# First layer of a two-block transformer on one core: order of the modulation slabs, early loads and turnings changed

## The reference

```python
mod_x = (jax.nn.silu(c) @ w_ada[l] + b_ada[l])[:, None, :]          # w_ada: 1024 x 6144
mod_c = (jax.nn.silu(c_ctx) @ w_ada[l] + b_ada[l])[None, None, :]
sh_a, sc_a, g_a, sh_m, sc_m, g_m = jnp.split(mod_x, N_MOD, axis=-1)
hx = _modulate(_rmsnorm(x, norm_attn[l]), sh_a, sc_a)               # h * (1 + scale) + shift
hc = _modulate(_rmsnorm(cx, norm_attn[l]), csh_a, csc_a)            # the context, 256 rows
qa, ka, va, qb, kb, vb, ga, gb = proj(hx)                           # w_in: 1024 x 4352
cqa, cka, cva, cqb, ckb, cvb, cga, cgb = proj(hc)
# heads of q and k are normed and rotated; keys and values of x and context are joined
ya = _sweep_query_blocks(_gqa_attend, qa, ka_all, va_all)
yb = _sweep_query_blocks(lambda qq, kk, vv: _diff_attend(qq, kk, vv, lam), qb, kb_all, vb_all)
x = x + g_a * _merge(ya, yb, ga, gb, w_oa[l], w_ob[l], w_out[l])
hx = _modulate(_rmsnorm(x, norm_mlp[l]), sh_m, sc_m)
x = x + g_m * moe(hx.reshape(b * s, d)).reshape(b, s, d)            # 32 experts, top 4
```

## Time and profile before

| what | value |
|---|---|
| median of 3 runs | 1993.06 us (1991.01 to 1995.98) |
| profiled execution | 1986.67 us, span 1984.9 us, mean granted clock 0.979 |
| PE busy | 1817.4 us, 92% |
| VectorE busy | 773.5 us, 39% |
| ACT busy | 600.0 us, 30% |
| chain that ended last | PE 57%, DMA 32% (nearly all of it the experts' `w_up`) |
| moved from HBM | 560.58 MB, 283 GB/s over the span |

### The profile page before, as it was taken

One profiled execution on the slowest core, in us unless ns is written; L12 is line 12 of the kernel. 1 busy time (PEld: TensorE's weight loads), 2 busy tenths in 40 slices (PEclk: granted clock), 3 DMA queues, 4 the chain that ended last, 5 costly groups with the idle time before them and its releaser, 6 DMA issues.

```text
span 1984.9 us, 24817 instructions
## 1 busy us (share of the span) xinstructions
PE 1817.4 (92%) x10349; PEld 1120.8 (56%) x10349; DVE 773.5 (39%) x1348; ACT 600.0 (30%) x1070; POOL 31.9 (2%) x67
## 2 busy tenths in 40 slices
PE   3799988899999999999999999979899998899999
PEld 3687767433333333333333333338689997778998
DVE  2465636322222222222231321234554455645544
ACT  3345553211101101111111110135554445555442
POOL 1300001000000000000000000000000000000000
PEclk9899999799999999999999999989999999999999
DMA  8420758299999999999999999975236454324551
GB/s 303 156 101 21 265 183 338 77 428 427 430 427 427 426 428 428 427 427 428 428 429 427 427 428 427 427 277 205 100 120 212 171 180 180 116 97 149 191 174 40
DMA packets 122051, 563.28 MB, mean 284 GB/s; under 512 B 7216, under 2 KB 53424, under 8 KB 97360
## 3 DMA queue, kind: packets, MB, share of 16 engines
q1 hardware_dynamic: 118352, 557.86, 70.1%
q10 hardware_dynamic: 3584, 3.79, 0.6%
HBM read 560.58 MB, written 1.05 MB: 283 GB/s over the span
## 4 chain that ended last, share of the span: by engine, by line
PE 57%; DMA 32%; DVE 4%; ACT 3%; issue 2%; ACTq 1%; SPq 0%; DVEq 0%
DMA ring<-in_w_up 32%; PE ps L984 13%; PE ps L617 12%; PE ps L618 11%; PE ps L619 11%; PE ps L642 1%; PE ps L1017 1%; DVE part L1856 1%; PE ps L1108 1%; PE ps L724 1%; ACT part L1341 1%; DMA ring<-in_w_ob 1%; PE ps L734 1%; DVE arena L1856 1%; SPq L605 0%
## 5 line engine op out<-in xcount | busy, mean ns | idle before, releaser
L617 PE MATMUL ps<-part,part 128*128 128x256 f32 (+2 forms) x1592 | 512.5, 322 | 16.0 <-DVE part L1856 14.5
L618 PE MATMUL ps<-part,part 128*128 128x256 f32 (+2 forms) x1592 | 504.2, 317 | 0.0
L619 PE MATMUL ps<-part,part 128*128 128x256 f32 (+2 forms) x1592 | 503.5, 316 | 0.0
L984 PE MATMUL ps<-ring,arena 128*64 128x512 f32 x2048 | 456.3, 598 | 51.0 <-DMA ring<-in_w_up 51.0
L1856 DVE TENSOR_TENSOR part<-ring,part 128x1024 fp32r<-128x1024 f32 (+2 forms) x299 | 313.3, 1090 | 150.0 <-ACT part L1341 149.6
L984 PEld LDWEIGHTS ps<-ring,arena 128*64 128x64 f32 x2048 | 155.4, 137 | 349.7 <-issue 349.7
L617 PEld LDWEIGHTS ps<-part,part 128*128 128x128 f32 (+1 forms) x1592 | 306.6, 193 | 47.5 <-issue 20.8
L619 PEld LDWEIGHTS ps<-part,part 128*128 128x128 f32 (+1 forms) x1592 | 305.8, 192 | 19.7
L618 PEld LDWEIGHTS ps<-part,part 128*128 128x128 f32 (+1 forms) x1592 | 306.4, 192 | 17.5
L1341 ACT ACTIVATE part<-ring 128x1024 fp32r<-128x1024 f32 (+2 forms) x299 | 271.7, 947 | 46.3 <-PE ps L619 23.9
L1853 DVE TENSOR_SCALAR arena<-ps 64x512 f32<-64x512 f32 x128 | 88.1, 688 | 399.3 <-PE ps L984 394.3
(11 more groups left out here) (247 smaller groups left out, 1012.9 us busy)
## 6 DMA issues: line engine op xcount, KB each, us to landing
ring<-in_w_gate SPq DMA_DIRECT2D x64, 2048.0 KB, 17.0
ring<-in_w_up SPq DMA_DIRECT2D x64, 2048.0 KB, 21.7
ring<-in_w_down SPq DMA_DIRECT2D x64, 2048.0 KB, 19.1
ring<-in_ffn_w_in SPq DMA_DIRECT2D x44, 1024.0 KB, 7.8
ring<-in_w_ada SPq DMA_DIRECT2D x12, 2048.0 KB, 8.4
ring<-in_ffn_w_out SPq DMA_DIRECT2D x10, 2048.0 KB, 7.9
ring<-in_w_in SPq DMA_DIRECT2D x8, 2048.0 KB, 11.0
ring<-in_a_w_in SPq DMA_DIRECT2D x6, 2048.0 KB, 12.4
```

The costliest lines, as they stand in the source:

```text
L617: e.matmul(out, x[0], y[0], start=first, stop=False, skip_group_check=True)
L618: e.matmul(out, x[0], y[1], start=False, stop=False, skip_group_check=True)
L619: return e.matmul(out, x[1], y[0], start=False, stop=last, skip_group_check=True)
L984: i = e.matmul(PS[p + h][CAP * r:CAP * r + CAP, :], xg[:, k0 + k, :], W(("moe_" + "gu"[r], ex, k0))[:, k, 512 * h:512 * h + 512], start=False,
```

## The change

- SP's list: slabs 1 and 3 come before `qa`; `ob` comes before slab 9, the first slab of `w_out` before slab 11; slots of `w_out`, the experts and the later stages are renamed.
- Products 9, 10 and 11 stand at steps 32, 35 and 37 (31, 33 and 35 before). The row for `g_a` is made at step 36 and in other banks.
- Products 1 and 3 stand together behind the first piece; the second piece of kva is the second step and not the fourth. PE waits for each low quarter of the modulated rows as it needs it.
- Product 0 stands in front of the turning of x, product 2 between those of x and of the context.
- ACT issues `par` first and only four loads; the six small ones are issued by SP behind `vb`. Silu comes first on ACT.
- The context is modulated by ACT, not POOL.
- Turnings of queries and keys are one step later (last number of a line of `procs`), and ACT makes its high half ahead of the root in steps that norm heads.

```diff
             if slot is None:
-                slot = (0, 3, 2, 1)[next(turn) % 4]
+                slot = (2, 3, 1, 0)[next(turn) % 4]
...
-        for key in (("ada", 0, 0), ("ada", 2, 1), ("in", "kva"), ("in", "qa"), ("ada", 1, 0), ("ada", 3, 1), ("in", "kb"), ("in", "qb"),
+        for key in (("ada", 0, 0), ("ada", 2, 1), ("in", "kva"), ("ada", 1, 0), ("ada", 3, 1), ("in", "qa"), ("in", "kb"), ("in", "qb"),
...
-                    ("ada", 7, 2), ("o", "oa", 1), ("ada", 8, 2), ("ada", 9, 2), ("ada", 10, 2), ("o", "ob", 0), ("ada", 11, 2),
-                    ("out", 0, 2), ("first", 0, 4), ("out", 1, 1)):
+                    ("ada", 7, 2), ("o", "oa", 1), ("ada", 8, 2), ("o", "ob", 0), ("ada", 9, 2), ("ada", 10, 2), ("out", 0, 1), ("ada", 11, 2),
+                    ("first", 0, 4), ("out", 1, 0)):
...
-            for k0, slots in ((0, (4, 0)), (4, (3, 5))):
+            for k0, slots in ((0, (4, 2)), (4, (3, 5))):
...
-            for k0, slot in ((0, 2), (4, 1)):
+            for k0, slot in ((0, 1), (4, 0)):
...
-        a_order = [("kva", 0), ("qa0", 0), ("qa1", 0), ("kva", 1), ("qa0", 1), ("qa1", 1)]
+        a_order = [("kva", 0), ("kva", 1), ("qa0", 0), ("qa1", 0), ("qa0", 1), ("qa1", 1)]
...
-        procs = [("kva", 0, 2, 1, 4, 5), ("kva", 1, 2, None, 4, 5), ("qa0", 0, 4, 0, 5, 6), ("qa1", 0, 4, 0, 6, 7), ("kb0", 0, 4, 3, 8, 9),
+        procs = [("kva", 0, 2, 1, 4, 6), ("kva", 1, 2, None, 4, 6), ("qa0", 0, 4, 0, 5, 7), ("qa1", 0, 4, 0, 6, 8), ("kb0", 0, 4, 3, 8, 10),
...
-        ada_step = {4: 20, 5: 23, 6: 25, 7: 27, 8: 29, 9: 31, 10: 33, 11: 35}
+        ada_step = {4: 20, 5: 23, 6: 25, 7: 27, 8: 29, 9: 32, 10: 35, 11: 37}
...
+                if key == ("in", "vb"):
+                    e.dma_start(bdn[:, :], A["b_down"][0]).then_inc(*s_small_ld.up("bdn"))
...
+                            if t < 6 and q == 0 and k % 2 == 0:
+                                e.wait_ge(*s_ulo.of("a", who, 2 * p + k // 2))
...
                 if u == 0:
-                    for i in (2, 3):
-                        e.wait_ge(*s_nte.of(i))
+                    e.wait_ge(*s_nte.of(7))
...
-                if t == 1:
+                if t == 0:
                     ada(1, 6)
-                if t == 2:
+                    ada(3, 7)
                     ada_columns(1, 6, a.rows[1])
-                    ada(3, 7)
                     ada_columns(3, 7, a.rows[3])
...
+            e.wait_ge(*s_par.of())
+            e.wait_ge(*s_zero.of())
+            e.activation(a.c32[:, :, 0:2], P("c2", 0, 16).rearrange("p (k t) -> p k t", t=2), ACT.Silu).then_inc(*s_silu.up())
+            e.preload_act_table(ACT.Sqrt)
...
+                for k in (2 * p, 2 * p + 1):
+                    n = e.activation(a.uT[:, 1, k, :], a.uT[:, 1, k, :], ACT.Identity, bias=M(0, k, 1), scale=a.ga1[:, 8 + k:9 + k])
+                n.then_inc(*s_umodc.up(p))
...
+                if now:
+                    high_a(t + 4)
                 for i in now:
                     heads_root(i)
```

More of the change, by code:

```diff
@@ L605, in sync_program @@
                     e.dma_start(to, src).then_inc(s_slot[slot].sem, 16)
+                if key == ("in", "vb"):
+                    e.dma_start(bdn[:, :], A["b_down"][0]).then_inc(*s_small_ld.up("bdn"))
+                    e.dma_start(rw[:, :, :], A["router_w"][0].rearrange("(k p) n -> p k n", p=128)).then_inc(*s_small_ld.up("rw"))
+                    e.dma_start(rb[:, :], A["router_b"].broadcast_to([128, NE])).then_inc(*s_small_ld.up("rb"))
+                    e.dma_start(wgt[:, :, :], A["a_w_in"][0].rearrange("(k p) n -> p k n", p=128)[:, :, 3072:3080]
+                                ).then_inc(*s_small_ld.up("wgt"))
+                    e.dma_start(pos[:, :], A["positions"]).then_inc(*s_small_ld.up("pos"))
+                    e.dma_start(par[:, PCOL["b_gate"]:NP], A["par"][:, PCOL["b_gate"]:NP]).then_inc(*s_small_ld.up("biases"))
             for q in range(2):
@@ L622, in part @@
                 return [x[:, at:at + n] for x in w]
-            e.wait_ge(*s_con.of())
-            for who, rows in enumerate((X, a.cx)):
-                for q in range(2):
-                    e.wait_ge(*s_diag.of("first", who, q))
-                    for j in range(2):
-                        if who:
-                            e.wait_ge(*(s_urawd if j else s_uraw).of(0, q))
-                        for k in range(4):
-                            i = e.matmul(PS[2 * q + j][:, 128 * k:128 * k + 128], rows[:, q, 512 * j + 128 * k:512 * j + 128 * k + 128],
-                                         a.first_diag[who][q], start=True, stop=True, skip_group_check=True)
-                        i.then_inc(*s_ut.up("first", who, q, j))
             def ada(s, bank):
@@ L654, in tensor_program @@
             ada(0, 4)
-            ada(2, 5)
+            e.wait_ge(*s_con.of())
+            for who, rows in enumerate((X, a.cx)):
+                for q in range(2):
+                    e.wait_ge(*s_diag.of("first", who, q))
+                    for j in range(2):
+                        if who:
+                            e.wait_ge(*(s_urawd if j else s_uraw).of(0, q))
+                        for k in range(4):
+                            i = e.matmul(PS[2 * q + j][:, 128 * k:128 * k + 128], rows[:, q, 512 * j + 128 * k:512 * j + 128 * k + 128],
+                                         a.first_diag[who][q], start=True, stop=True, skip_group_check=True)
+                        i.then_inc(*s_ut.up("first", who, q, j))
+                if who == 0:
+                    ada(2, 5)
             ada_columns(0, 4, a.rows[0])
@@ L1388, in u_high, with context_mod @@
                 copy(u_of[who][:, 0, 2 * p:2 * p + 2, :], a.uT[:, who, 2 * p:2 * p + 2, :]).then_inc(*s_uhi.up("a", who, p))
-            ada_row(0, 4, a.rows[0])
-            ada_row(2, 5, a.rows[2])
-            high_a(0)
-            for who in range(2):
-                for p in range(2):
-                    u_high(who, p)
-            high_a(1)
-            ada_row(1, 6, a.rows[1])
-            high_a(2)
-            ada_row(3, 7, a.rows[3])
-            high_a(3)
-            high_a(4)
-            for who in range(2):
-                for p in range(2, 4):
-                    u_high(who, p)
-            for t in range(5, 8):
+            def context_mod(p):
+                e.wait_ge(*s_gain.of(p // 2))
+                if p >= 2:
+                    for q in range(2):
+                        e.wait_ge(*s_urawd.of(1, q))
+                else:
+                    e.wait_ge(*s_uraw.of(1, 1))
+                for k in (2 * p, 2 * p + 1):
+                    n = e.activation(a.uT[:, 1, k, :], a.uT[:, 1, k, :], ACT.Identity, bias=M(0, k, 1), scale=a.ga1[:, 8 + k:9 + k])
+                n.then_inc(*s_umodc.up(p))
+            for g in range(2):
+                ada_row(g, 4 + 2 * g, a.rows[g])
+                ada_row(2 + g, 5 + 2 * g, a.rows[2 + g])
+                high_a(g)
+                for p in (2 * g, 2 * g + 1):
+                    context_mod(p)
+                    u_high(0, p)
+                for p in (2 * g, 2 * g + 1):
+                    u_high(1, p)
+            for t in range(2, 8):
                 high_a(t)
@@ L1498, in scalar_program @@
                     e.preload_act_table(ACT.Sin)
-                if t + 4 < 50:
+                if t + 4 < 50 and not now:
                     high_a(t + 4)
@@ L1905, in vector_program @@
                     n.then_inc(*s_umod.up(p))
-                low_a(3 * g)
+                low_a(g)
                 for who in range(2):
@@ L1909, in vector_program @@
                         u_low(who, p)
-                if g == 0:
-                    low_a(1)
-                    low_a(2)
-            for t in range(4, 8):
+            for t in range(2, 8):
                 low_a(t)
```

50 lines of the change are left out of this document (15 added, 35 removed).

## The result

The changed kernel takes 1972.69 us (median of four runs, 1971.33 to 1973.61) against 1992.03 us for the kernel before beside it (1987.5 to 1996.0). The ratio is 0.9903, 95% interval 0.9881 to 0.9926: 19 us faster, where 15 were forecast. The profiled execution of the changed kernel took 1973.61 us, its span is 1971.6 us; the span before was 1984.9.

A forecast was written before the change was run, and what follows sets the result against it. Experts' weight loads bound 387 to 1297 us and only shift with PE's first layer; 17.9 + 2.6 - 5.2 = 15.3 us off 1986.67 gives 1971.4, carried to a median of 1978 us, range 1964 to 1988.

The forecast's parts named there:

- Start: PE's start: bound moves from ACT's queue to slab 0, landing at 17.3; first projection piece at 36.1 against 46.19.
- Rival (b): At the start, only 9 to 10 us of gain stay, giving 1988 us; chance 0.19 together with (d).
- Second half of the modulation: kva's second half at 53.8, not 74.35 (20.5 us); kb at 73.7 against 91.8; 17.9 us gained so far, start included.
- Turnings: Turning keys and queries a step later removes 3.3 us of PE's waits, less 0.7 at first attention: 2.6 us gained.
- Rival (c): VectorE's two normed-row buffers make it wait for later turnings, costing PE about 30 us: 2008 us; chance 0.06.
- Small loads and POOL: Small loads on SP may hold it 15 us, and ACT modulates the context instead of POOL: nothing gained or lost.
- Late products: ob's wait and slow product go (10.3 us); waits of 4.8 and 7.4 at slabs 9 and 11 come: 5.2 us lost.
- (a): The late slabs don't end last, so the gain is 30.8 us and the time 1962 us; chance 0.17.
- (d): ob is still late and its 8.6 us wait stays as well: 1988 us; chance 0.19 together with Rival (b).
- the last line of the sum: Carries the profiled execution's 1971.4 us to a median of 1977.8, as the earlier profile was 6.4 us under its median.

The follow-up runs named there:

- small_on_act: The changed kernel with its six small loads moved from SP back to ACT's queue, behind the four first ones: 1981.14 us, ratio 0.9950 to the kernel before.
- second_old: The changed kernel with the second half of the modulation, its loads and piece order as before: 1978.39 us, ratio 0.9948 to the kernel before.
- turn_back: The changed kernel with keys and queries turned one step sooner, as before: 1973.80 us, ratio 0.9916 to the kernel before.
- late_only: The kernel before with only the change's late part (order of late loads, products 9 to 11, gain row) laid on it: 1996.48 us, ratio 1.0036.
- early_only: The changed kernel with its late part (order of late loads, products 9 to 11, gain row) undone: 1967.36 us, ratio 0.9881 to the kernel before.
- late_mended: The changed kernel with two pairs in SP's list swapped, slab 9 ahead of ob and slab 11 ahead of out's first slab: 1958.51 us, ratio 0.9838.
- ctx_later: late_mended with ACT asking for the context only when x and the constants have landed: 1956.92 us, ratio 0.9822 to the kernel before.

## Why the prediction was right, step by step

The forecast was 1978.0 us with a range of 1964 to 1988; 1972.69 lies in it, nearer to the lower part. The forecast's case came true (a gain at the start and in the second half, two new late waits), and the size was 5 us short. That it was no further off is in part luck: the last bullet and the paragraph behind it name errors that stand against each other.

- **Start.** Slab 0 was the bound, as said, but it landed at 15.4 and not 17.3. First block 34.62 for a forecast of 36.1: 11.6 us gained instead of 10.1. By the sum's own terms it was 36.4: 32.2 and 4.8 (41.36 to 46.19), less 0.65. Slab 0 alone would have brought 1.9 us more; the turnings took 4.0 and 3.8 us and not 3.6 each, and from the modulation to the block it was 3.3 us. small_on_act shows what most of the gain hangs on: with the small loads back on ACT 7.8 us are lost at the first block. Rival (b), half a gain, fell.
- **Second half of the modulation.** kva's second half at 52.1 (forecast 53.8), the wait before kb 0.88 (0.8), kb0's block at 72.63 (73.7). The steps are right to 1.7 us. By itself this part is worth 7 us at kb0 (second_old), close to the 17.9 less 10.1 of the sum. The prediction was right to put only 1.28 us on ACT's table: in small_on_act the silu ends at 22.32, the load runs from 22.34 for 1.28 us, and the square starts at 23.63. The 1380 ns of drain that the Trainium skill (ScalarE: Activation LUTs, section "What ACT_TABLE_LOAD costs") adds to a switch do not show there.
- **Turnings.** PE waits for none. From kb1's block on (79.73 for 99.71) to the wait at L742 (167.44 for 190.25) the gain grows by 2.8 us; 2.6 were forecast. The share given to the later step alone was too large: with the high half ahead of the root, 1.6 us of waits were left for it (turn_back), not 3.3. Rival (c), VectorE's two buffers, cost PE nothing: VectorE waited for a turning once, 3.5 us, and was far enough ahead.
- **Small loads and POOL.** Nothing was forecast and nothing is seen: SP is held at three of them for 8.6, 4.8 and 3.5 us from 53.9 on, and ga0 follows at 74.3, at about the time when its slot comes free.
- **Late products.** Waits of 4.39 and 7.02 us (forecast 4.8 and 7.4), landings 13.3 and 13.4 us behind the issue (13.7), two slow products. The gain falls from 24.4 us (the scores at 201.75 for 226.12) to 18.8 at the turning of rows, by 5.6 for a forecast of 5.2. late_only and early_only put it at 5 to 7 and at 5 us. This is the step that the forecast had to get against the purpose of the edit, and it did. Rivals (a) and (d) fell with it.
- **Not foreseen.** The router's matmuls took 7.0 us for 3.9, the last expert's took 8.80 us for 7.10, and 0.7 went in smaller pieces, so that of 18.8 us 13.3 were left in the span.

**The step that failed is the last line of the sum**: "it was 6.4 us under the median of the three runs, which carries to 1977.8". It takes for granted that the changed kernel's executions lie above their profile's sum by as much. The sum gave 1971.4 us for a profiled execution, and 1973.61 was measured: 2.2 us too little, since the 3.5 us that the first layer gained above the sum went again, and more, at the router and behind it. But that execution stands 0.9 us above its kernel's median and not 6.4 below it. The two errors, 7.3 and 2.2 us, have opposite signs, and 5.1 is what is left of them.

Why the carry failed is shown for one pair of executions. The second profile of the kernel before was 5.0 us longer than the first: net 1.3 us up to the turning of rows, 3.1 at the router. The changed kernel's profile had the slow router, as all others had; and at the other place, the piece behind 3.01 us of waiting, the changed kernel has no wait behind which PE's clock could fall (that it can lose nothing there is argued from this and not measured). By the spans the change is worth 13.3 us against the first profile of before and 18.3 against the second (1989.9 less 1971.6), and by the medians 19.

## What to carry to other kernels

A load's place in its queue is to be set by when it is wanted, not by what else is ready to be asked for: of two 2 MB loads asked for within half a microsecond the first landed after 8 us and the second after 13, a load that waits for its slot holds back the one behind it, and two swapped pairs were worth 14 us here. Before a single profile's sum is carried to a median, look for short waits behind which PE ran at full clock: here two executions of one kernel differ by 1.1, 2.4 and 3.1 us at three of them (product 4, the piece between products 1 and 3, the router), and a wait that is removed can give back the slow work behind it too (1.7 us at each late product). And a gain read at one instruction is not a gain until it is read again where the moved work has been made up for: the 11.5 us of the new order at kva's second half were 6.9 at kb0's block.

## What the runs showed of the hardware

- Six small loads behind four large ones on ACT hold it for 9.7 and 5.6 us at two issues, 15.2 us in all, though the two move 32 KB and 1 KB; on SP, behind larger loads, three of the same six held it for 8.6, 4.8 and 3.5 us.
- Slab 0 was not slowed by what stood behind it in its own queue (there at 15.2 and 15.4 with slab 2 asked for at once or 4.3 us later), but by the other queue's bytes (13.55 with 1 MB less there).
- Of two 2 MB loads asked for 0.4 us apart in one queue the first landed after 8.2 us and the second after 13.1 (ob and slab 9); out's first slab and slab 11 took 8.0 and 13.2.
- Behind waits of the same length in the same code PE's granted clock was 1.00 in one execution and partly 0.5 in another. At product 4, behind a wait of 2.45 us, the product took 1.92 us in late_mended and 2.80 in ctx_later, the matmuls behind it were slow too, and all of ctx_later's lead of 1.3 us was gone. What decides it was not tried.
- The router's matmuls took 401 ns each in thirteen of the fourteen profiles and 276 ns in the first one of the kernel before alone. The four waits in front of them are the same in both profiles of the kernel before (0.59, 1.27, 3.31 and 0.60 us); what made that one fast stays open.
